# Router constants before the gate's wait, deviations in row tiles, and an attention norm in two column parts

## The reference

```python
# layer 1, end of the time mixing: o is normalised per head of 64, scaled, gated, projected
mu = o.mean(-1, keepdims=True)
var = jnp.square(o - mu).mean(-1, keepdims=True)
o = ((o - mu) * lax.rsqrt(var + LNX_EPS)).reshape(B, T, D) * lnx[0] + lnx[1]
o = o + (jnp.sum(rh * kh * r_k, -1, keepdims=True) * vh).reshape(B, T, D)
out = (o.astype(x.dtype) * g) @ w_out

# layer 2, end of the attention: o is normalised per head of 128, scaled, projected
o = o * lax.rsqrt(jnp.mean(jnp.square(o), -1, keepdims=True) + SUBLN_EPS) * subln
o = o * (1.0 - lambda_init)
return o.reshape(B, T, D_MODEL).astype(x.dtype) @ w_out

# after both: residual, layer norm, router, experts
x = _layernorm(DEEPNORM_ALPHA * x + h, post_ln[l, 0, 0], post_ln[l, 0, 1])
s = jax.nn.sigmoid((xt @ router_w).astype(f32))
sel = s + router_b.astype(f32)
for e in range(N_EXPERTS):
    h = jax.nn.silu(xt @ w_gate[e]) * (xt @ w_up[e])
    y = y + gates[:, e:e + 1] * (h @ w_down[e])
```

## Time and profile before

| what | value |
|---|---|
| median of 3 runs (lowest to highest) | 1184.09 us (1183.66 to 1185.23) |
| the profiled execution: its time, its span | 1182.83 us, 1181.0 us |
| busy: PE, PEld, DVE, ACT, POOL | 1053.4, 733.8, 532.8, 361.4, 70.2 us |
| chain that ended last, by engine | PE 74%, DVE 11%, DMA 7%, ACT 3% |
| of it, two lines of DMA | `in_moe_w_up` 5%, `in_router_b` 1% |
| DMA moved | 273.80 MB, mean 232 GB/s |

### The profile page before, as it was taken

One profiled execution on the slowest core, in us unless ns is written; L12 is line 12 of the kernel. 1 busy time (PEld: TensorE's weight loads), 2 busy tenths in 40 slices (PEclk: granted clock), 3 DMA queues, 4 the chain that ended last, 5 costly groups with the idle time before them and its releaser, 6 DMA issues.

```text
span 1181.0 us, 23944 instructions
## 1 busy us (share of the span) xinstructions
PE 1053.4 (89%) x10417; PEld 733.8 (62%) x10418; DVE 532.8 (45%) x1042; ACT 361.4 (31%) x730; POOL 70.2 (6%) x101
## 2 busy tenths in 40 slices
PE   4989988898989399999998899999779699999994
PEld 3967988888857354545443899877446544444531
DVE  5857456566664641212123744575344621222215
ACT  3435534443432421111101534463323311111112
POOL 2002010011001000000000112202000000000000
PEclk8999989999989799999999899999989799999998
DMA  9512020013023969999999605444834299999992
GB/s 331 204 40 61 12 67 4 3 40 110 12 72 115 396 247 423 422 422 422 424 422 391 258 1 190 178 178 151 324 110 157 88 397 423 422 423 422 423 410 78
DMA packets 57165, 273.80 MB, mean 232 GB/s; under 512 B 5169, under 2 KB 5690, under 8 KB 32994
## 3 DMA queue, kind: packets, MB, share of 16 engines
q1 hardware_dynamic: 47136, 237.58, 50.1%
q0 software_dynamic: 9296, 34.33, 8.9%
q10 hardware_dynamic: 626, 0.32, 0.1%
HBM read 265.78 MB, written 6.46 MB: 231 GB/s over the span
## 4 chain that ended last, share of the span: by engine, by line
PE 74%; DVE 11%; DMA 7%; ACT 3%; issue 2%; DVEq 1%; POOL 0%; SPq 0%; POOLq 0%; ACTq 0%
PE ps L764 67%; DMA arena<-in_moe_w_up 5%; ACT arena L1580 1%; PE ps L905 1%; DMA arena<-in_router_b 1%; PE ps L1468 1%; DVE arena L2047 1%; DMA arena<-in_cache_k 1%; PE ps L1341 1%; DVE pwr_lo L2053 1%; PE ps L1176 1%; ACT arena L1583 1%; DVE arena L2346 1%; DVE arena L2185 1%; PE ps L1293 1%
## 5 line engine op out<-in xcount | busy, mean ns | idle before, releaser
L764 PE MATMUL ps<-arena 64*64 64x64 f32 (+14 forms) x7572 | 599.6, 318 | 43.4 <-DVE arena L2533 10.8
L764 PEld LDWEIGHTS ps<-arena 64*64 64x64 f32 (+6 forms) x7572 | 330.5, 138 | 288.7 <-issue 226.8
L1583 ACT COPY arena<-ps 128x512 f32<-128x512 f32 (+7 forms) x304 | 125.3, 433 | 307.6 <-PE ps L764 157.1
L2428 DVE TENSOR_TENSOR arena<-arena,ps 128x512 f32<-128x512 f32 x16 | 17.4, 1085 | 165.5 <-PE ps L764 165.5
L1580 ACT ACTIVATE arena<-ps,arena 128x256 f32<-128x256 f32 (+5 forms) x97 | 45.9, 505 | 125.8 <-PE ps L764 96.6
L2439 DVE SCALAR_TENSOR_TENSOR yy_lo<-ps,arena,yy_hi 128x512 fp32r<-128x512 f32 x32 | 22.7, 747 | 123.0 <-ACT yy_hi L1580 123.0
L1580 ACT ACTIVATE pw_hi<-arena 128x1024 fp32r<-128x1024 f32 x40 | 42.1, 1057 | 90.9 <-PE ps L764 90.9
L764 PE MATMUL ps<-px_hi,pw_hi 128*128 128x336 f32 x192 | 63.0, 328 | 2.5 <-DVE px_lo L2267 1.4
L764 PE MATMUL ps<-px_lo,pw_hi 128*128 128x336 f32 x192 | 61.5, 320 | 0.0
L764 PE MATMUL ps<-px_hi,pw_lo 128*128 128x336 f32 x192 | 61.4, 320 | 0.0
L1580 ACT ACTIVATE yy_hi<-ps,arena 128x512 fp32r<-128x512 f32 x32 | 20.5, 684 | 106.3 <-PE ps L764 106.3
(11 more groups left out here) (229 smaller groups left out, 1384.4 us busy)
## 6 DMA issues: line engine op xcount, KB each, us to landing
arena<-in_moe_w_gate SPq DMA_DIRECT2D x64, 1024.0 KB, 15.8
arena<-in_moe_w_up SPq DMA_DIRECT2D x64, 1024.0 KB, 19.2
arena<-in_moe_w_down SPq DMA_DIRECT2D x64, 1024.0 KB, 18.7
arena<-in_rwkv_w_rkv SPq DMA_DIRECT2D x6, 2048.0 KB, 19.4
arena<-in_w_kv_shared SPq DMA_DIRECT2D x4, 2048.0 KB, 19.7
arena<-in_cache_k POOLq DMA_DIRECT2D x16, 512.0 KB, 4.6
arena<-in_cache_v POOLq DMA_DIRECT2D x16, 512.0 KB, 6.7
arena<-in_rwkv_w_out SPq DMA_DIRECT2D x2, 2048.0 KB, 10.0
```

What stands on the lines that cost most here:

```text
L764: return pe.matmul(out, lhsT, rhs, start=start, stop=stop)
L1583: return act.copy(out, in_)
L2428: tt(HH.rearrange("p (k q) -> p q k", k=NF), HS.rearrange("p (q k) -> p q k", k=NF), bank(3).rearrange("p (q k) -> p q k", k=NF), ALU.mult ...
```

## The change

- POOL: `mconst`, `rw` and `rbB` of layer 1 are loaded right after the constants of the group norm, at the end of the recurrence, ahead of the wait for `z_ready` 8. For that they get a place of their own in `arena`.
- TensorE, end of layer 1: the first four deviations are issued in a row, from four groups of 32 partitions, into banks 6, 7, 4 and 5; the other four in two pairs after steps 0 and 1; the last four gates in two pairs after steps 2 and 3. The last chunk's `new_state` moves from ahead of the first deviation to after step 5, and the eight matmuls of the state to after step 6. Two groups of four small matmuls of the mean become one matmul each.
- VectorE, end of layer 1: the multiply with the deviation becomes a step of its own, `scaled(c)`, that runs up to four blocks ahead of `gated(c)`; state sum and decay go to the end.
- Layer 2's norm in two parts. The 256 prompt columns: squares on ScalarE within units 2 to 5, a load of the root's table and a dummy root at unit 8, sums on TensorE ahead of unit 9's values, root and reciprocal after that. The 80 other columns after the last unit. The sums now go to four column tiles of 32, so that each block's scale is spread from its own 32 partitions, four in a row into banks 6, 7, 4 and 5. The factor is folded into the gain once.
- The order of splits in layer 2's projection: `wide_hi` and `wide_lo` stand between pairs of blocks and no longer behind all eight.
- The second half of layer 1's `w_out` lands in slot 3 and not 0; which slots SP's expert loads wait for changes with it.

```diff
@@ experts' slots and weights on SP
-            return {5: 0, L_WO: 4, L_WO + 1: 0}.get(n, n % NSLOT)
+            return {5: 0, L_WO: 4, L_WO + 1: 3}.get(n, n % NSLOT)
-                    sp.wait_ge(S("st_mm"), NCH - 1)
+                    sp.wait_ge(S("st_mm"), NCH - 2)
-                        if layer == 0 and i == 2:
-                            sp.wait_ge(S("pw_lo"), 4)
+                        if layer == 0 and i in (1, 2):
+                            sp.wait_ge(S("pw_lo"), 8)
-                        if layer == 0 and i >= 4:
-                            sp.wait_ge(S("pw_lo"), 8)
@@ POOL
             ld(gconst, cd[:, heads0:heads0 + 512], "in_rows")
+            ld(mconst, cd[:, mconst0:mconst0 + nM], "in_mconst")
+            ld(rw, I["router_w"].rearrange("(c p) n -> p c n", p=P), "in_mconst")
+            ld(rbB, I["router_b"].unsqueeze(0).to_broadcast([P, E_]), "in_mconst")
...
             pool.wait_ge(S("z_ready"), after("z_ready", 8))
             gains(0, 0)
-            ld(mconst, cd[:, mconst0:mconst0 + nM], "in_mconst")
-            ld(rw, I["router_w"].rearrange("(c p) n -> p c n", p=P), "in_mconst")
-            ld(rbB, I["router_b"].unsqueeze(0).to_broadcast([P, E_]), "in_mconst")
@@ TensorE, layer 1
             gate(2, 0, "gu_mm")
-            new_state(NCH - 1)
+            pe.wait_ge(S("gr_ready"), after("gr_ready", 1))
+            for c, b in enumerate((6, 7, 4, 5)):
+                deviations(c, b, "gr_mm")
             pe.wait_ge(S("bu_ev"), after("bu_ev", 1))
-            bonus(6, 2, "gu_mm")
-            pe.wait_ge(S("gr_ready"), after("gr_ready", 1))
-            for c in range(2):
-                deviations(c, 6 + c, "gr_mm")
+            bonus(6, 2, "gv_mm")
...
+                if k < 2:
+                    pe.wait_ge(S("y_read"), 2 * k + 4)
+                    for i in range(2):
+                        deviations(4 + 2 * k + i, 6 + i, "gx_mm")
+                elif k < 4:
+                    for i in range(2):
...
+                        gate(2 * k + i, 6 + i, "gx_mm")
                 elif k == 5:
+                    pe.wait_ge(S("z_ready"), after("z_ready", 7))
+                    new_state(NCH - 1, 6)
+                elif k == 6:
+                    pe.wait_ge(S("st_ready"), NCH - 1)
@@ TensorE, layer 2
+                if i == UNITS - 1:
+                    pe.wait_ge(S("in_rows"), 32)
+                    head_squares(0)
                 unit_values(i)
             turn_out(UNITS - 1)
-            for c in range(NC):
-                pe.wait_ge(S("sl_sq"), after("sl_sq", c + 1))
-                m = mm(ps[0:H, 0, 0:T], sum_rows("rows2", c), aSQ[:, c, :], c == 0, c == NC - 1)
+            pe.wait_ge(S("sl_sa"), after("sl_sa", 1))
+            head_squares(1)
...
+            def scales(k):
+                if k < 0:
+                    for c, b in enumerate((6, 7, 4, 5)):
+                        scale(c, b)
+                elif k < 2:
+                    for c in (4 + 2 * k, 5 + 2 * k):
+                        pe.wait_ge(S("z2_ready"), after("z2_ready", c if k else c - 3))
+                        scale(c, 6 + c % 2)
@@ ScalarE, layer 2
+                if 2 <= i < 6:
+                    two = slice(2 * i - 4, 2 * i - 2)
+                    f(aSQ[0][:, two, :], aOT[:, two, 0:256], ACT.Square).then_inc(S("sl_sqa"), 1)
+                if i == UNITS - 2:
+                    f(st4[0][:, 6:7], eps_ln, ACT.Sqrt)
+                if i == UNITS - 1:
+                    act.wait_ge(S("sl_mm"), after("sl_mm", 1))
+                    f(anorm[:, 0:256], ps[:, 0, 0:256], ACT.Sqrt, scale=1.0 / P, bias=eps_ln).then_inc(S("sl_sa"), 1)
```

More of the change, by code:

```diff
@@ L127, in constants @@
     parts["odd"] = (p // SS) % 2
-    j = np.arange(H)[None, :]
-    parts["rows"] = np.concatenate([j == 2 * c + p // 64 for c in range(NC)], 1)
-    parts["rows2"] = np.concatenate([np.broadcast_to(j // 2 == c, (P, H)) for c in range(NC)], 1)
-    parts["spread"] = np.concatenate([p == 2 * c + q // 64 for c in range(NC)], 1)
+    parts["pair"] = np.concatenate([np.broadcast_to(j // 16 == v, (P, 32)) for v in range(2)], 1)
+    parts["pairspread"] = np.concatenate([np.broadcast_to(p % 32 == 16 * v, (P, P)) for v in range(2)], 1)
     at, out = {}, []
@@ L350, in build @@
         aconst0 = at["caus"][0]
-        nA = at["rows"][0] - aconst0
+        nA = at["pair"][0] - aconst0
         aconst = cut(nA)
@@ L360, in build @@
         st4 = [cut(8) for _ in range(2)]
[L361 to L364 removed]
+        aSQ = [cut(NC * 256, pp_at).rearrange("p (c n) -> p c n", c=NC),
+               cut(NC * 80, pp_at + NC * 256).rearrange("p (c n) -> p c n", c=NC)]
+        rows0 = at["pair"][0]
         nN = const.shape[1] - rows0
@@ L1153, in out_proj @@
                             if t < 2:
-                                pe.wait_ge(S("gv_ev"), after("gv_ev", t + 1))
+                                pe.wait_ge(S("gv_ev"), after("gv_ev", t + 2))
                             else:
-                                pe.wait_ge(S("st_ready"), NCH - 1)
+                                pe.wait_ge(S("y_read"), 4)
+                        if place == 1 and k == 0 and t == 2:
+                            pe.wait_ge(S("z2_ready"), after("z2_ready", 4))
                         for hf in range(2):
@@ L1536, in turn_out, with head_squares @@
                 m.then_inc(S("s_ot"), 1)
+            def head_squares(part):
+                name, per, cols = (("sl_sqa", 2, slice(0, 256)), ("sl_sqb", 4, slice(256, T)))[part]
+                for c in range(NC):
+                    if c % per == 0:
+                        pe.wait_ge(S(name), after(name, c // per + 1))
+                    m = mm(ps[tiles[c % 4], 0, cols], nconst[:, 32 * (c // 4):32 * (c // 4) + 32], aSQ[part][:, c, :], c < 4, c >= 4)
+                m.then_inc(S("sl_mm"), 1)
             for i in range(NU + 3):
@@ L1887, in _ @@
             copy(T1[:, 2, :], bank(0, T)).then_inc(S("gu_ev"), 1)
-            act.wait_ge(S("gu_mm"), after("gu_mm", 2))
-            copy(rT[:, 6, :], bank(2, T)).then_inc(S("gu_ev"), 1)
+            for c in range(2):
+                act.wait_ge(S("gv_mm"), after("gv_mm", c + 1))
+                copy(rT[:, 6 + c, :], bank(2 - c, T)).then_inc(S("gv_ev"), 1)
             for c in range(2):
@@ L1995, in _ @@
                 copy(OB[i % 2], bank(6, 256)).then_inc(S("ob_ready"), 1)
-            act.wait_ge(S("s_oev"), UNITS)
-            for c in range(NC):
-                f(aSQ[:, c, :], aOT[:, c, :], ACT.Square).then_inc(S("sl_sq"), 1)
-            act.wait_ge(S("sl_mm"), after("sl_mm", 1))
-            f(norm16, ps[0:H, 0, 0:T], ACT.Sqrt, scale=1.0 / P, bias=eps_ln[0:H]).then_inc(S("sl_s"), 1)
             act.wait_ge(S("out_ktm"), 64)
@@ L2003, in _ @@
             wide_hi(1, 1, L_DO, 0)
-            wide_hi(1, 1, L_DO, 1)
+            act.wait_ge(S("s_oev"), UNITS)
+            for j in range(2):
+                f(aSQ[1][:, 4 * j:4 * j + 4, :], aOT[:, 4 * j:4 * j + 4, 256:T], ACT.Square).then_inc(S("sl_sqb"), 1)
+            act.wait_ge(S("sl_mm"), after("sl_mm", 2))
+            f(anorm[:, 256:T], ps[:, 0, 256:T], ACT.Sqrt, scale=1.0 / P, bias=eps_ln).then_inc(S("sl_s"), 1)
             for c in range(NC):
@@ L2007, in _ @@
                 px_hi(1, aOT, c)
-            for k in range(2, NC):
+                if c % 2:
+                    wide_hi(1, 1, L_DO, (c + 1) // 2)
+            for k in range(5, NC):
                 wide_hi(1, 1, L_DO, k)
```

170 lines of the change are left out of this document (88 added, 82 removed).

## The result

The changed kernel took 1164.43 us in the median of four executions (1161.39 to 1169.07), the kernel before 1183.88 beside it: a ratio of 0.9842, interval 0.9809 to 0.9875, so 18.7 us (14.8 to 22.6) faster. Run again later it gave 0.9801 (0.9766 to 0.9837). The prediction was 1161.0 in 1153 to 1169. The profiled execution took 1163.61 us with a span of 1161.6, 19.4 less than before.

What follows compares the result with a forecast made beforehand. The end was taken to hang on layer 1's residual, through gather and expert-weight stream, and in layer 2 on small steps between last unit and projection. 1182.83 less 12.5 (layer 1) and 9.3 (layer 2) gave 1161.0 us, range 1153 to 1169.

Steps and rivals of the forecast that it cites:

- The bound: Layer 1's residual, through gather and restart of expert loads, moves the end one for one; seven slots leave 15 us room.
- Constants, 7.5: End of layer 1: router constants loaded early end the residual's wait for them, 7.62 us less 0.15, so 7.5 gained.
- Layer 1's product, 5.1: Layer 1's projection: row tile 0 done at 377.2 instead of 382.29, 5.1 us gained, bounds 2.5 and 7.5.
- 31 us from residual to gather: Layer 1's routing: the stretch behind the residual stays as long with early constants, at most 0.15 us different.
- layer 1's 12.5: Layer 1's total gain: 7.5 for constants plus 5.1 for the product, taken as 12.5 us.
- One of the signs by which the prediction was to be wrong: Expert loads on SP not restarting 12 us earlier; the forecast had them restart at about 417.
- Units, -1.45: Layer 2's units: added squares cost 0.2 us; table load, dummy root and sums delay the last `unit_out` by 1.25.
- Last unit to projection, 9.5: Layer 2, last unit to projection: 15.07 us falls to 5.6, a gain of 9.5 before the units' 1.25.
- Steps 0 and 1 of layer 2, 1.35: Start of layer 2's projection: 16.45 us falls to 15.1 including one TensorE wait, 1.35 gained, bounds -1.5 and 4.5.
- become the bound in layer 1: Rival: VectorE's multiplies make it late in three of the first steps, 1.5 us each: 1165.5, chance 0.15.
- The slower case: Rival: TensorE's clock stays at 0.50 through both projections, 288 matmuls costing 0.2 us more each: 1218, chance 0.05.
- The better case: Rival: no low-clock spells, three of 1.6 us, and no wait after step 1, 2.9: 1153.3, chance 0.12.

Runs made afterwards that it cites:

- the run with the constants alone: Kernel before the change, with only layer 1's router constants loaded early in a place of their own: 1175.94 us, ratio 0.9933.
- the run with the order alone: Kernel before the change, with layer 1's new order of deviations, state and gates, constants still loaded late: 1174.94 us, ratio 0.9909.
- the scale wait: Changed kernel, layer 2's last pair of scales waiting only for the multiply that frees its bank, one block earlier: 1153.47 us, ratio 0.9759.
- the run with the short fill: Changed kernel with the scales' shorter wait, idle matmuls around layer 2's norm, and nine plus two in layer 1's routing: 1155.03 us, ratio 0.9746.

## Why the prediction was right, and where its terms were off

- **The bound.** That the residual's shift reaches the end, through the restart of the loads, holds in each trace: from the restart to layer 2's first projection matmul of keys the 14 traces are within 227.6 to 228.1, but for the two in which the wait at the branch brought the low clock (229.7 and 229.8). There was room in the seven slots, though less than reckoned: in the first trace the loads moved until about 407 and not 401.5 (0.61 of the stretch 405 to 408, nothing from 408 to 414), and restarted at 420.36.
- **Constants, 7.5:** 7.3 by the run with them alone.
- **Layer 1's product, 5.1:** from the reciprocal's end it came 42.78 us later and not 49.93: 7.15. But 1.4 of these belong to the profiled execution of the kernel before, which had a second low-clock spell, in step 2. The run with the constants alone has the same order and does not have it; the first block shows the first two matmuls of that step in the profiled execution before, the second block those of the run with the constants alone:

```profile
351.47 1.10 PE L764 MATMUL ps<-pw_hi,px_hi 128*128 128x512 f32 x1
352.38 0.63 PE L764 MATMUL ps<-pw_hi,px_lo 128*128 128x512 f32 x1
```

```profile
354.36 0.65 PE L767 MATMUL ps<-pw_hi,px_hi 128*128 128x512 f32 x1
354.84 0.39 PE L767 MATMUL ps<-pw_hi,px_lo 128*128 128x512 f32 x1
```

In that run the residual comes 48.64 after the reciprocal, and 42.89 with the new order: 5.75, near the 5.1. Start of the projection 1.35 earlier (1.6 taken); the rest is in the steps. The sum kept the low-clock spell of 1.6 that the earlier trace rows show in step 0. All three traces with the old order have it (5.78 to 5.90 from the first matmul to the deviations behind step 0), none of the eleven with the new one (4.29 to 4.33). A pair of deviations cost 0.95 (342.26 - 337.16, less 18 matmuls of 0.23), with 1.15 taken; a pair of gates 1.1 (1.4 taken).
- **"31 us from residual to gather", the step that failed in the profiled execution:** 34.52, and 1.6 more to the restart. It is 30.49 in the kernel's second trace. The row was right for the kernel and the spread between executions was missing: layer 1's 12.5 came out as 14.3 at the residual and 9.2 at the restart. Rows of two routings had shown no long kind, so no bound held it. One of the signs by which the prediction was to be wrong, loads that don't restart 12 us earlier, was there in this execution.
- **Units, -1.45:** -0.81 in this trace; -3.33 in the kernel's second one, behind a long wait for the cache's pages. The squares in units 2 to 5 cost nothing that shows, the table load 0.72. The idle time of a drain of 1.4 us that the Trainium skill ("ScalarE: Activation LUTs", section "What ACT_TABLE_LOAD costs") adds is not in this trace either: ScalarE's instruction ahead of the load ends at 837.29 and the load starts at 837.31; it ends at 838.59 and the next ACTIVATE starts at 838.61.
- **Last unit to projection, 9.5:** 9.26. Here too the clock of an execution has a part: in the run with the order alone, whose layer 2 is the old one, the stretch took 13.37 and not 15.07, as the sums over partitions ran at the full clock there:

```profile
855.21 4.68 PE L762 MATMUL ps<-arena 128*16 128x336 f32 x16 [0.92 <-ACT arena L1584]
```

The same row took 6.37 in the profiled execution before. Against the shorter one the change is worth 7.6.
- **Steps 0 and 1 of layer 2, 1.35:** 849.28 to 865.01 are 15.73, so 0.72. The sum has 9.8 for two steps that it prices at 5.8 and 4.2, so it was 0.2 too good. The stall was of the kind worked out, 2.12 long and not 3.15 plus 0.4; against it 13 matmuls at the low clock in step 0, where 8 were taken. Together layer 2 gave 9.2 by these three stretches, with 9.3 predicted.
- **Rivals.** VectorE did not become the bound in layer 1: TensorE is busy without a gap from 340 to 375. The rule of the Trainium skill, "TensorEngine Tiling (Array Packing)", section "PSUM Bottleneck", that the reads of PSUM may become the limit, is not borne out by this trace. The slower case did not come: the low clock of step 0 in layer 2 ended within the step. The better case was half there, as layer 1's projection had no spell, and the wait after step 1, which it wanted gone, was the one wait whose removal paid (the scale wait, 4.7).

That the total was met to 3 us owes something to luck: in this execution two errors cancel in part, 1.8 too little up to the residual and 5.1 too much behind it, and the execution it is held against had low clock in two places (1.4 and 1.7 us) where another execution of the same code had none.

## What to carry to other kernels

When a bank passes from one block to the next, count the wait on the read that frees the bank, not on the latest block in program order: one count too many cost 4.6 to 4.8 us here, by way of another engine. Where an execution-to-execution spread of some us exists, cut the traces at the same events and compare stretches, and look at more than one trace of each kernel before a stretch is taken as fixed. Idle matmuls held the clock here, and no time showed a gain from them; they must be shorter than the gap, and by making the program longer they moved a branch to a place where it took 6 us.

## What the runs showed of the hardware

- TensorE's granted clock in the routing came back at different times in executions of one kernel: 0.50 until 414 in the first trace, 1.00 from 408 in the second, which started the stretch 4.7 us later. With idle matmuls in layer 1's gaps it was 1.00 through the gathers in three traces of three; in layer 2 it had fallen to 0.51 and 0.53 where such a fill began, and was 1.00 before its end.
- An idle matmul of 336 float32 columns took about 0.58 us in a row (nine and four small ones took 5.64 in the run with the short fill); a gate of the same shape had been read as 0.44 from a pair (0.88 from its start to the next step's).
- One branch in TensorE's program, in layer 1, took its sequencer 6.1 to 6.5 us in the three traces with seventeen more matmuls ahead of it, wherever these stood, and 0.37 to 0.39 in the ten with none and the one with eleven. TensorE stood 2.9 to 3.3 us of that. The layer ended 1.9 later where the clock fell behind the wait, 0.3 later where it did not. In layer 2 the same branch took from 0.3 to 3.5 us and did not follow the count.
- An ACT_TABLE_LOAD followed directly by its ACTIVATE: 1.28 us, with 0.02 behind it.
